# Two transformer blocks on one core: tokens loaded alone, norm rows and two expert chunks moved in the queues, block masks copied by ScalarE

## The reference, cut to what matters

```
h = layer_norm(x, ln_in_g, ln_in_b)
proj = h @ w_in                        # 1024 x 5120: q, k, v of two attentions, and gates
out_a = diff_attention(...)            # 4 heads of 2 x 64
out_b = chunk_band_attention(..., rel_bias)   # 8 heads of 64, a relative bias
m = (gate0 * (out_a @ w_branch_a) + gate1 * (out_b @ w_branch_b)) @ w_out
h = layer_norm(2**0.25 * h + m, ln1_g, ln1_b)
f = sum over each token's 4 of 32 experts: swiglu(h @ w_exp_in[e]) @ w_exp_out[e]
x = layer_norm(2**0.25 * h + f, ln2_g, ln2_b)
# second block: adaLN from c_2, a convolution and a gated linear recurrence,
# an MLP, stick-breaking attention, an MLP
```

## Time and profile before

| | us |
|---|---|
| median of 3 runs (1847.04 to 1848.11) | 1847.23 |
| the profiled execution | 1847.14 |
| its span | 1845.4 |
| PE busy in the span | 1743.0 (94%) |
| DVE busy | 799.8 (43%) |
| ACT busy | 504.1 (27%) |
| POOL busy | 88.7 (5%) |

### The profile page before, as it was taken

The page is one execution under the profiler, slowest core; times in us unless marked ns, Lnnn a source line. Parts: engine busy times, 40 slices in busy tenths (PEclk is TensorE's granted clock), DMA queues, the critical chain, the costliest instruction groups (busy, mean ns, idle before and its releaser), DMA issues. The chain is left out here.

```text
span 1845.4 us, 23805 instructions
## 1 busy us (share of the span) xinstructions
PE 1743.0 (94%) x9717; PEld 1066.1 (58%) x9718; DVE 799.8 (43%) x1123; ACT 504.1 (27%) x648; POOL 88.7 (5%) x101
## 2 busy tenths in 40 slices
PE   6999999999999989999899989899899999999999
PEld 6874764333433323333233323597799988568998
DVE  6878652212211212121121212566864467766454
ACT  4325411000010000001000000434644454555442
POOL 7400000000000000000000000202000000000000
PEclk9999999999999999999999999999999999999999
DMA  9779899999999999999999999864465545776551
GB/s 302 284 263 320 294 401 427 427 428 428 427 427 427 428 427 429 427 428 428 427 428 428 427 428 427 318 211 165 160 229 186 192 147 184 275 273 206 190 193 49
DMA packets 134512, 598.12 MB, mean 324 GB/s; under 512 B 17472, under 2 KB 17632, under 8 KB 109584
## 3 DMA queue, kind: packets, MB, share of 16 engines
q1 hardware_dynamic: 126336, 589.35, 80.7%
q10 hardware_dynamic: 7280, 5.25, 1.0%
q0 software_dynamic: 800, 2.11, 0.4%
HBM read 595.58 MB, written 1.11 MB: 323 GB/s over the span
## 5 line engine op out<-in xcount | busy, mean ns | idle before, releaser
L175 DVE TENSOR_TENSOR wl<-raw,wh 128x2048 fp32r<-128x2048 f32 x125 | 284.7, 2308 | 78.8 <-ACT wh L169 78.6
L169 ACT ACTIVATE wh<-raw 128x2048 fp32r<-128x2048 f32 x126 | 237.0, 1914 | 161.0 <-PE banks L217 101.7
L1532 DVE COPY hid<-banks 128x512 f32<-128x512 f32 x32 | 22.1, 692 | 509.9 <-PE banks L1479 509.9
L252 PE MATMUL banks<-xth,wh 128*128 128x256 f32 x800 | 224.7, 281 | 4.5 <-DVE xtl L690 3.6
L252 PE MATMUL banks<-xtl,wh 128*128 128x256 f32 x800 | 224.2, 280 | 0.0
L252 PE MATMUL banks<-xth,wl 128*128 128x256 f32 x800 | 224.1, 280 | 0.0
L1479 PE MATMUL banks<-moe_halves,xs 128*64 128x512 f32 x832 | 188.1, 597 | 10.5 <-DMA moe_halves<-in_w_exp_in 10.5
L252 PEld LDWEIGHTS banks<-xth,wh 128*128 128x128 f32 x800 | 151.0, 189 | 5.5 <-issue 4.6
L252 PEld LDWEIGHTS banks<-xth,wl 128*128 128x128 f32 x800 | 150.9, 189 | 0.0
L252 PEld LDWEIGHTS banks<-xtl,wh 128*128 128x128 f32 x800 | 150.6, 188 | 0.3
L1479 PEld LDWEIGHTS banks<-moe_halves,xs 128*64 128x64 f32 x832 | 56.4, 137 | 127.9 <-issue 100.3
(11 more groups left out here) (408 smaller groups left out, 2327.6 us busy)
## 6 DMA issues: line engine op xcount, KB each, us to landing
moe_halves<-in_w_exp_in SPq DMA_DIRECT2D x52, 2048.0 KB, 42.1
raw<-in_mlp_w SPq DMA_DIRECT2D x64, 1024.0 KB, 6.0
moe_left<-in_w_exp_in SPq DMA_DIRECT2D x26, 2048.0 KB, 41.2
raw<-in_w_exp_in SPq DMA_DIRECT2D x25, 2048.0 KB, 43.4
moe_halves<-in_w_exp_out SPq DMA_DIRECT2D x24, 2048.0 KB, 44.6
raw<-in_ada_w SPq DMA_DIRECT2D x38, 1024.0 KB, 6.9
moe_gates<-in_w_exp_in SPq DMA_DIRECT2D x13, 2048.0 KB, 41.6
raw<-in_w_exp_out SPq DMA_DIRECT2D x13, 2048.0 KB, 44.5
```

The costliest lines, as they stand in the source:

```text
L169: act.activation(c.wh[:, slot], c.raw[:, slot], ACT.Copy).then_inc(c.high_ready, 1)
L175: dve.tensor_tensor(c.wl[:, slot], c.raw[:, slot], c.wh[:, slot].bitcast(F32), ALU.subtract).then_inc(c.low_ready, 1)
L252: mm = pe.matmul(out, w[:, slot, k, cols], x[:, k0 + k, :], start=first and k == 0 and j == 0 and b % 2 == 0, stop=last and k == CK - 1 an ...
L1532: dve.tensor_copy(c.hid[:, 1, :], c.bank[hid_banks(c, par) + 1]).then_inc(it.up_kept, 1)
```

## The change

- Start: chunk 0 is asked for only when both token tiles have landed, chunk 1 when chunk 0 has, chunk 2 when chunk 1 has; chunk 3 follows at once. `c_2` moves behind the norm rows. GpSimd's 16 loads of `rel` wait for chunk 3. VectorE splits chunk 0 in two halves, the second behind the first `xtl`.
- End of attention: expert chunk 1 is asked for when all units are biased, expert chunk 0 when all are kept, between the loads of `w_out`; then the `ln1` rows, now in SyncE's queue. The adaLN bias rows move from `va` to `acts`. The last two chunks of `w_out` no longer wait for the stored adaLN rows.
- The `ln2` rows move from ScalarE's queue at the start of the experts to SyncE's, between the two `gap` chunks.
- Recurrence: the predicated copies of levels 6 and 7 become plain copies of the blocks by ScalarE (two of 32 x 8 x 32, one of 64 x 8 x 64).

```diff
 def multiply_cols(...)
-    pe.wait_ge(half or c.low_ready, 1 if half else n + 1)
+    if half is None:
+        pe.wait_ge(c.low_ready, n + 1)
+    else:
+        pe.wait_ge(c.first_low, half)
...
             for n in range(LOADED):
-                if n == 1:
-                    sp.wait_ge(x_loaded[TT - 1], 16)
+                if n == 0:
+                    for m in range(TT):
+                        sp.wait_ge(x_loaded[m], 16)
+                if n in (1, 2):
+                    sp.wait_ge(c.arrived[n - 1], 16)
                 if n == RING:
                     sp.wait_ge(c.xl_ready, KT // 2)
...
-                if n == 2:
+                if n == RING:
                     sp.wait_ge(c.rs_ready, 1)
...
             pool.wait_ge(rel_stored, 16)
+            pool.wait_ge(c.arrived[RING - 1], 16)
             for h in range(HB):
...
-            split_low(c, dve, W, 0)
+            split_low_half(c, dve, W, 0, c.first_low)
             for b in range(KT // 2):
+                if b == 1:
+                    split_low_half(c, dve, W, 1, c.low_ready)
                 if b == 2:
...
+def load_first(c, sp, n):
+    layer, e, which = first_chunks()[n]
+    w = c.dram["w_exp_in" if layer == 1 else "w_exp_out"][0, e]
+    sp.dma_start(c.moe_ring.slots[n], (first_rows if layer == 1 else second_rows)(w, which)
+                 ).then_inc(c.moe_ring.arrived[n], 16)
...
+            sp.wait_ge(biased, units)
+            load_first(c, sp, 1)
             for n in range(after + 4, after + LOADED):
                 load_chunk(c, sp, W + n, n % RING, rows_cols(d["w_out"][0], 0, n % 2 * COLS))
+                if n == after + 4:
+                    sp.wait_ge(kept, units)
+                    load_first(c, sp, 0)
+            for j, name in enumerate(("ln1_g", "ln1_b")):
+                sp.dma_start(norm[:, j, :], d[name][0].partition_broadcast(P)).then_inc(c.ln_loaded, 16)
...
+            for n in range(LOADED, after):
+                load_chunk(c, sp, W + n, n % RING, rows_cols(w_out, 512, n % 2 * COLS))
             sp.wait_ge(c.mod_stored, first.stored)
             sp.wait_ge(c.mod_turned, 1)
-            for n in range(LOADED, after):
-                expert(n - LOADED)
-                load_chunk(c, sp, W + n, n % RING, rows_cols(w_out, 512, n % 2 * COLS))
             sp.wait_ge(merged, 4)
...
                 sp.dma_start(gap[:, n], ada_source(c, 1, n)).then_inc(gap_loaded[n // 2], 16)
+                if n == 0:
+                    for j, name in enumerate(("ln2_g", "ln2_b")):
+                        sp.dma_start(c.ln2[:, j, :], d[name][0].partition_broadcast(P)).then_inc(c.ln2_loaded, 16)
...
+            def keep_blocks(l):
+                w = WIDTHS[l]
+                act.wait_ge(c.paired, l + 1)
+                act.wait_ge(masked, l)
+                for at in range(0, P, 2 * w):
+                    x = act.activation(
+                        c.h[at:at + w, 0].rearrange("p (n t) -> p n t", n=8)[:, :, at + w:at + 2 * w],
+                        c.psum[at:at + w, 2 * (l % 2):2 * (l % 2) + 2, :].rearrange(...)[
+                            :, :, at + w:at + 2 * w], ACT.Copy)
+                x.then_inc(masked, 1)
             for l in range(3, levels):
                 decay_act(c, act, l)
+                if l - 1 in BLOCK_LEVELS:
+                    keep_blocks(l - 1)
```

More of the change, by code:

```diff
@@ L500, in phase_in @@
     cols_turned = c.sem("in_cols_turned")
+    c.first_low = c.sem("first_low")
     evacuated = c.sem("in_evacuated")
@@ L777, in _ @@
                     n = 2 * p + h
-                    (multiply_cols if kinds[p] == "T" else multiply_rows)(
-                        c, pe, W + n, n % RING, h * CK, c.bank[p % 2 * 2:p % 2 * 2 + 2], h == 0, h == 1,
-                        turn=0 if p == 0 else None)
+                    if p == 0:
+                        multiply_cols(c, pe, W + n, n % RING, h * CK, c.bank[0:2], h == 0, h == 1, turn=0,
+                                      half=1 if h == 0 else None)
+                    else:
+                        (multiply_cols if kinds[p] == "T" else multiply_rows)(
+                            c, pe, W + n, n % RING, h * CK, c.bank[p % 2 * 2:p % 2 * 2 + 2], h == 0, h == 1)
                 for m in range(given_last(p - 1) // PANEL, given_last(p) // PANEL):
@@ L813, in phase_attend @@
     sub_step = c.sem("sub_step")
+    c.ln_loaded = c.sem("ln1_loaded")
     block = c.block
@@ L826, in phase_attend @@
         ss = c.sb("ss", [P, TT, HA], ctx=local)
-        part = c.first_part = ModPart(c, 0, 0, FIRST_MOD, 7, c.va[0:FIRST_MOD, 0, :], a[:, 0].rearrange("p j s -> p (j s)"), "mod0a_")
+        norm = c.qka[:, :, :, :].rearrange("p j h s -> p j (h s)")
+        part = c.first_part = ModPart(c, 0, 0, FIRST_MOD, 7, c.acts[0:FIRST_MOD, :, :].rearrange("p k s -> p (k s)"), a[:, 0].rearrange("p j s -> p (j s)"), "mod0a_")
         part.early = part.given = GIVEN
@@ L1082, in _ @@
         def _(sp):
[L1083 to L1087, removed]
+            for n in range(LOADED, after):
+                load_chunk(c, sp, W + n, n % RING, rows_cols(w_out, 512, n % 2 * COLS))
             sp.wait_ge(c.mod_stored, first.stored)
             sp.wait_ge(c.mod_turned, 1)
-            for n in range(LOADED, after):
-                expert(n - LOADED)
-                load_chunk(c, sp, W + n, n % RING, rows_cols(w_out, 512, n % 2 * COLS))
             sp.wait_ge(merged, 4)
-            expert(2)
+            load_first(c, sp, 2)
             for j in range(2):
                 sp.wait_ge(c.low_ready, W + after - RING + 2 * j + 2)
-                expert(7 + j)
+                load_first(c, sp, 7 + j)
             for j in range(2):
                 sp.wait_ge(c.used, W + after - RING + 2 * j + 2)
-                expert(3 + 2 * j)
-                expert(4 + 2 * j)
-            expert(9)
+                load_first(c, sp, 3 + 2 * j)
+                load_first(c, sp, 4 + 2 * j)
+            load_first(c, sp, 9)
         @block.gpsimd
@@ L1121, in _ @@
                 split_high(c, act, W + n, (W + n) // RING + 1, n % RING)
-            for j, name in enumerate(("ln1_g", "ln1_b")):
-                act.dma_start(norm[:, j, :], d[name][0].partition_broadcast(P)).then_inc(ln_loaded, 16)
             act.dma_start(wr[:, :, :], d["w_router"][0].rearrange("(k p) e -> p k e", p=P)).then_inc(ln_loaded, 16)
@@ L1695, in _ @@
             load_spill(act, "act")
-            for j, name in enumerate(("ln2_g", "ln2_b")):
-                act.dma_start(c.ln2[:, j, :], d[name][0].partition_broadcast(P)).then_inc(c.ln2_loaded, 16)
             act.wait_ge(weight_turned, 1)
@@ L2074 @@
 WIDTHS = (0, 1, 2, 4, 8, 16, 32, 64, 128)
+BLOCK_LEVELS = (6, 7)
 def halves(t, w):
@@ L2402, in _ @@
                         multiply_cols(c, pe, n, n % RING, h * CK, panel_banks(p), h == 0, h == 1, turn=entry.turn,
-                                      ready=BOTH_TILES, half=first_low if h == 0 else None)
+                                      ready=BOTH_TILES, half=2 if h == 0 else None)
                     else:
@@ L2497, in _ @@
                     mask(0)
-                if s >= 3:
+                if s >= 3 and s - 2 not in BLOCK_LEVELS:
                     mask(s - 2)
```

7 lines of the change are left out of this document (4 added, 3 removed).

## The result

The change makes the kernel slower: 1855.12 us, median of 5 runs (1854.48 to 1855.60), against 1847.23. The ratio is 1.0043 with a 95% interval of 1.0031 to 1.0054, so +7.9 us. The forecast was 1850.7 with a range of 1843.5 to 1854.0: right in sign, too small by 4.4 us, and the time is outside the range. The profiled execution took 1854.48 us with a span of 1852.6 (before: 1845.4).

The account below looks back on a forecast made before the run. The experts were taken as bound by DMA at 428 GB/s, the stages around them by the engine chain, with chunk 4's landing critical in phase_in. Sum: 1847.1 + 6.0 (chunk 4) - 2.5 (`ln2`) + 0 = 1850.7 us, range 1843.5 to 1854.0.

Parts of the forecast that it names:

- Start: Up to the first product: it moves from 19.67 to about 19.1 us, worth at most 0.6 us.
- The failed step, chunk 4: In phase_in, chunk 4 lands at 43.5 us beside `rel` and norm rows; TensorE gets chunk 6 6.0 us later.
- From the landing to chunk 6: In phase_in, 17.6 us of work in a row from chunk 4's landing to the end of chunk 6's split.
- GpSimd and the second `given`: GpSimd's masks move 16 us, second `given` asked for at 84.7; chunk 14 still in time, cost nothing, 8 us spare.
- End of attention: End of attention and merge: expert chunks 0 and 1 land sooner, hidden by the routing; 0 us.
- `ln2`: Experts: the rows leave the full stream, -2.5 us; their return behind the last expert chunk is hidden.
- Recurrence: Two masks of 1.3 us leave VectorE without effect on the time: 0, between -0.5 and +0.5 us.
- 1: Phase_in: milder mixture, chunk 4 lands at 39.0, cost +1.5 us, sum 1846.1; chance 0.17.
- 4: Expert stream starts sooner, since the queue's backlog sets it: 6.5 us won, 1844.2; chance 0.08.
- 2: GpSimd late, SyncE stands at the second `given`; TensorE waits 3.5 us at chunk 14: 1854.2; chance 0.10.
- Rival 3: Phase_in: VectorE holds up GpSimd's requests, chunk 4 passes them and lands 1.9 us sooner: 1848.8; chance 0.12.

Follow-up runs that it names:

- a_cols_behind: Changed kernel with the single-number loads (`c_2`, norm column) asked for behind chunk 5 instead of ahead of chunk 4: 1852.40 us, ratio 1.0026.
- b_rel_wait: Kernel before with only GpSimd's wait for chunk 3 ahead of the `rel` loads added: 1850.78 us, ratio 1.0022.
- a_busy30: Changed kernel with 30 idle identity products on TensorE ahead of chunk 4: 1856.49 us, ratio 1.0050.
- a_early4: Changed kernel with chunks 4 and 5 asked for right behind chunk 3, ahead of norm rows, `c_2` and norm column: 1847.04 us, ratio 1.0008.
- b_zero: Kernel before with the early expert chunks 0 and 1 and `ln1` rows, and ScalarE's block copies: 1847.19 us, ratio 1.0002.
- a_no_serial: Changed kernel without the waits of chunks 1 and 2 for the chunk before; the wait for the tokens stays: 1850.12 us, ratio 1.0017.
- a_rel_free: Changed kernel with GpSimd's `rel` loads asked for at once, without the wait for chunk 3: 1853.09 us, ratio 1.0035.
- b_ln2: Kernel before with only the move of the `ln2` rows: 1845.54 us, ratio 0.9992.

## Why the prediction was wrong

The path was right up to chunk 4: `rel` and the norm rows beside it make chunk 4 late, and TensorE waits for it. Three terms of the sum failed: the landing of chunk 4 was put 2.0 us too early, the way from there to chunk 6 0.6 us too short, and the cover over the `ln2` rows, forecast as whole, cost 1.2 us.

- **Start.** Chunk 0 at 14.2 (14.18), first product at 19.1 (19.13), chunk 1 at 19.2 (19.23), chunk 3 at 27.0 (27.10): as forecast. That the 0.6 us are worth nothing is right too: they go into the wait for chunk 4. They are hardly there to begin with. Kernels in which VectorE splits chunk 0 whole have the first product at 18.94 to 19.67, those with the start of the change at 19.05 to 19.29. That chunk 3 ends at the same time in the two traces compared (last product at 43.77 and 43.85) is chance: the slow pace of 0.21 us lasted 3.7 us before and 4.8 in the change, but 2.9 to 4.8 in five executions with the same new start, and in four of them chunk 3 ended sooner, with its last product at 42.9 to 43.4.
- **The failed step, chunk 4.** "I take 43.5, near the upper end", with 44.0 for all of it in: it was 45.46. I had SyncE ask for chunk 4 at 28.8. It asked at 31.05, since the issues of `c_2` and the norm column took 2.85 us, where the same two took 0.80 before. From the asking to ScalarE's start the forecast had 14.7 us, and it took 14.4 (15.2 in a_cols_behind, 15.3 in b_rel_wait). So what failed is the time of asking: it came 2.25 us late, and the two issues that made it late stand nowhere in the sum; a_cols_behind asks at 28.25 and has chunk 4 2.0 us sooner. Over the whole stretch the rate was nearly right: 4.2 MB at 369 GB/s and 3.2 us for the single numbers are 288 GB/s, and 279 were moved from 28 to 44 us. Its course was not: 240 GB/s from 28 to 36 at a DMA share of 0.97, then 319. The row of 369 GB/s was mostly of a time after GpSimd's last request, at 20.03; the nearer neighbour was the 206 GB/s of 13 to 18 us, when GpSimd was asking, and I used that row for the price of `c_2` alone.
- **From the landing to chunk 6.** Forecast 17.6 us, measured 63.70 - 45.46 = 18.24. I took VectorE's chain as what decides, with a wait of TensorE at chunk 6. VectorE started the split of chunk 6 at 60.10, ready for it by 62.4, 16.9 us behind the landing; TensorE came at 63.70, with the low clock behind its own wait. Without that clock VectorE would have decided (a_busy30: 17.17), so 1.1 us of the 18.24 are the clock's. A forecast of a 6 us wait should have held a sentence on this term: the earlier trace rows had the granted clock of 0.72 at 20 to 26 us. Together with chunk 4: +8.6 instead of +6.0.
- **GpSimd and the second `given`.** 83.28 against 84.7, and chunk 14 was not waited for: right. a_early4 shows how thin that cover is: without the late chunk 4 GpSimd's lateness costs 1.3 us, at the sum over the second `given`.
- **End of attention.** 0, right (b_zero).
- **`ln2`.** -2.4 in the stream, as forecast. That the end hides them was wrong, by 1.2 us. I asked when VectorE wants the rows and not what is behind them in SyncE's queue. VectorE got them in time; the second `gap` load and the first `w_in_ab` chunk did not come in time for TensorE and ScalarE.
- **Recurrence.** 0, right: +7.35 ahead of it and +7.35 behind it.

The sum with what was measured: 1847.1 + 8.6 - 2.4 + 1.2 - 0.2 (a load of `ada_w` in the chain that ended last, near 1617 us before, takes 9.54 instead of 9.79) = 1854.3, against 1854.5.

Of the rivals, 1 is out (chunk 4 was later than forecast, not sooner), 4 is out (b_zero), and 2 did not decide here. Rival 3, with the rule of the Trainium skill, "SBUF — State Buffer", beside it, has nothing for it in these runs: GpSimd's sixteen requests took 8.52 us in the change, while VectorE was busy 5.54 of the 8 us from 28 to 36, and 9.02 before. Whether one of VectorE's instructions there was of the two-port kind isn't shown, so the rule itself isn't tested. The transfer's figure of the Trainium skill, "DMA: Bandwidth & Descriptors", anatomy of one DMA, 4.4 us for 1 MiB as an estimate and fitted on GpSimd's queue, is too low for SyncE's loads here: the shortest of the first 60 us took 5.0 us in this trace as well, the shortest of all 4.9.

## What to carry to other kernels

A load's place in the queue's program order is a resource of its own. Before loads are made to wait for each other to make room, look at which of them stands behind a wait that has nothing to do with it: moving two issues ahead of such a wait brought back the 8.6 us that the new waits had lost in this stage.

Asking costs time too. The issues of two small loads took 0.80 us before and 2.85 in the change, and chunk 4 behind them was asked for 2.25 us later than forecast.

One trace of each kernel is one execution. Before a difference of 1 us between two traces is explained, look at a third and a fourth that have the same code up to that place.

When a load is moved from a full stretch to the end of it, ask what stands behind it in the new queue, and not only who wants the load itself.

## What the runs showed of the hardware

- The sixteen `rel` loads of GpSimd's queue, with nothing else asked for, moved 104 GB/s at a DMA share of 0.71 (a_no_serial, 24 to 27 us), and with two loads of 1024 single numbers landing and no `rel` in flight the rate was 68 GB/s at 0.87 (a_rel_free, 38 to 40; 2014 of the 2053 packets were under 512 bytes). With both and the norm rows it was 240 at 0.97 (the change, 28 to 36; 232 to 265 in four other executions with this start), 245 with chunks 4 and 5 behind the norm rows (a_cols_behind) and 370 at 1.04 with chunk 5 ahead of them (a_early4). What decides between these isn't shown.
- A load of 4 KB in single numbers can hold its issuing queue. The issue of the norm column took 0.43 us in the kernel before, 1.01 in the change, 3.88 in a_no_serial, 8.76 in a_early4 and 13.32 in a_cols_behind, where two chunks stood ahead of it; that of `c_2` took 0.37 before and 1.84 in the change. Two row loads of 512 KB at the end of the experts' stream took 9.30 and 4.24 us to issue, where the two norm rows at 27 us took 0.34 and 0.43.
- After the first product TensorE kept a pace of 0.21 us for a length that changes from execution to execution: 4.8, 3.7, 2.9, 3.1 and 4.6 us in five with the same start (first product at 19.05 to 19.29), 3.7 and 5.7 before and in b_zero. In b_ln2 and b_rel_wait the first products came every 0.12 us, and the slow pace began 1.2 to 1.3 us later. The column of the granted clock doesn't always show it: 0.50 and 0.66 in 20 to 24 us before, 1.00 in the change at the same pace of the products.
